# Two blocks in f32: the last expert's rows added by TensorE, scores between query tiles, and the residual's last addition moved ahead

## The chip, the cores and the metric

One core of one Trainium2 chip runs the kernel. The metric is the device time of one execution in microseconds, lower is better. The kernel before took 2692.67 us (median of 3 runs, 2691.4 to 2695.11).

## The reference, cut to what matters

Everything is f32, 256 tokens of 1024 features. Two layers of a hybrid mixer, a cross-attention to a memory of 256 rows and a feed-forward part (dense in layer 0, eight experts with the best two per token in layer 1); then a second block (mLSTM, linear recurrence, and a retrieval of 16 x 8 single-neuron experts per token).

```python
def memory_cross_attention(xn, memn, w_xq, w_xkv, w_xo):     # 4 heads of 256
    q = (xn @ w_xq).reshape(bsz, s, X_HEADS, X_HEAD_DIM)
    k, v = jnp.split(memn @ w_xkv, 2, axis=-1)
    ...
    scores = jnp.einsum("bshd,bmhd->bhsm", q, k).astype(jnp.float32) * (X_HEAD_DIM ** -0.5)
    p = jax.nn.softmax(scores, axis=-1).astype(v.dtype)
    o = jnp.einsum("bhsm,bmhd->bshd", p, v).reshape(bsz, s, D_MODEL)
    return o @ w_xo

def moe_swiglu(xn, w_router, w_gate, w_up, w_down):
    ...
    for e in range(N_EXPERTS):
        y = y + combine[:, e:e + 1] * swiglu(xt, w_gate[e], w_up[e], w_down[e])

h = h + memory_cross_attention(rmsnorm(h, norm_x_g[layer]), ...)
h = h + (swiglu(...) if layer % 2 == 0 else moe_swiglu(...))      # then rmsnorm, second block
```

## The kernel before, in words

The residual `hF` lies transposed in SBUF: features on partitions, 8 tiles (`KT`) of 128 features by 256 tokens. Every engine has its own program, written out by hand, and they meet in semaphores. TensorE's program (`pe`) is the first to be written; the class `Groups` numbers its accumulation groups, hands out the eight PSUM banks in two rings of four ("v" banks emptied by VectorE, "a" banks by ScalarE), and remembers for each group the count at which it is done (`G.after`), the count at which it is taken (`G.took`), and which weight tile had been used by then (`G.tiles_at`). `G.begin` makes TensorE wait until the group four back in the same ring was taken.

Weights come in tiles of 1 MB, in a ring of seven, by SP's queue in the order in which they are used; a tile's load waits for the use of the tile seven before it. For most matrices a product is made of three: ScalarE rounds the tile to its high part (`round_ahead`, line 1489), VectorE subtracts to get the low part (`low_ahead`, line 1986), and TensorE multiplies high by high, low by high and high by low (`split_group`, lines 644, 645, 648; 48 matmul records for a group of 256 outputs). `round_ahead(key)` and `low_ahead(key)` first do every such tile up to `AHEAD` = 2 tiles behind the group `key`; they stand in front of the wait for that group, so the engine does tiles while TensorE works on it. An f32 matmul that is not split shows as two records.

**Attention** (`attention(l)` in each engine's program, both layers). TensorE: sums of squares, the last key-value tile, four query groups, then the four heads' scores (line 782), four groups of transposes of the probabilities, four output groups (line 794), then the output matrix `xo`. ScalarE copies the query groups to `qF` (line 1628), then for each head waits for the maximum and writes the exponentials with their sums (line 1641). VectorE takes the four maxima (lines 2174, 2175), then normalises head by head (2179, 2181), then copies the transposed probabilities (2187). Before the maxima it does `low_ahead((("q", l), 3))`.

**Residual.** `add_to_residual(key, follow)` on VectorE: per group g the low parts ahead, `follow(g - 1)`, then the addition of the group (line 2003). For `xo` the function to follow is `gained_low_parts` in layer 0 (low parts of the normalised input of the feed-forward, line 2025) and `gained_tokens` in layer 1 (line 2017). On ScalarE, `norm` squares each pair of tiles as it is added (line 1520), in layer 0 with the high parts of the scaled input (1523), and first does `round_ahead((h_key, g))`. TensorE sums the squares (line 554).

**Experts.** The tokens of an expert are listed by a matmul (buffer `lists`: tokens, shares and destination rows), POOL gathers their rows from `x_tokens` in DRAM, and TensorE transposes them; all this for the next expert while the current one runs. Behind the down projection ScalarE writes `ye` (tokens of this expert by 1024 features, scaled by their shares, line 1733), and POOL adds it to `y_tokens` in DRAM by an indirect DMA with an add (line 1449, signal `y_done`). `pick` is the one-hot matrix of tokens and places of the next expert; `weighted_now` is a copy of it made for the current one. After the last expert SP waits for `y_done` of all eight, reads 256 rows back (line 1370, `y_loaded`), TensorE transposes them in four groups, and VectorE adds them to the residual (line 2419). Then every engine skips the body of `If(overflow > 0)`, a second pass over all experts for lists longer than 128, and the second block starts: ScalarE's squares (1761), TensorE's sums (554), VectorE's `gain_sq` (2438), TensorE's sums with it (1009), VectorE's reciprocals (2445, 2450), rows of the next input (2453) and the first matrix (622). SP's next seven loads stand behind the read-back on its queue.

In the second block a padding transpose `pad_v` (VectorE's copy of it at 2636) is put in where the number of "v" groups so far is odd. The last stage is a run of 256 indirect gathers of rows by POOL, with row numbers in the buffer `work`.

## Time and profile before

| | us |
|---|---|
| median of 3 runs | 2692.67 |
| lowest, highest | 2691.4, 2695.11 |
| the profiled execution | 2696.5 |
| its span, to which all times of the trace refer | 2694.4 |
| busy in it: TensorE, VectorE, ScalarE, POOL | 2529.3, 2008.3, 1237.7, 286.4 |
| mean granted clock of TensorE | 0.975 |

A time in the trace counts from the span's start. The chain that ended last is followed back from the last instruction, at each step to what released it. "Issue" in it is time in which the engine waited for nothing that the profile shows. Matmuls overlap, so a record's length is more than the step from one to the next. The granted clock (PEclk) is 1.00 at 2.4 GHz and 0.50 at 1.2 GHz. In brackets stands how long the engine was idle before a row, and what released it.

### The profile page before, as it was taken

The page shows a single profiled execution, that of the slowest core. Times are in us where ns is not written, and L with a number is a line of the kernel's source. Part 1 is how long each engine was busy: PE and PEld are TensorE (multiplying, and loading weights), DVE is VectorE, ACT ScalarE, POOL GpSimd, SP SyncE. Part 2 cuts the span into 40 slices and gives each one's busy share as a digit, 9 for nine tenths or more (in the row PEclk, how much of TensorE's full clock was granted, in tenths as well). Part 3 has the DMA queues.
Part 4 walks back from the last instruction along what each step waited for, and adds up shares of the span by engine and source line. Part 5 has one row for each costly group of instructions (what it writes and reads, how often), then busy time and mean ns, then how long its engine had stood idle before and what let it go on. Part 6 is the DMA issues. An engine that isn't in the chain of part 4 may idle for free.

```text
span 2694.4 us, 33145 instructions
## 1 busy us (share of the span) xinstructions
PE 2529.3 (94%) x12345; PEld 1981.4 (74%) x12345; DVE 2008.3 (75%) x2983; ACT 1237.7 (46%) x1250; POOL 286.4 (11%) x303
## 2 busy tenths in 40 slices
PE   9999999999999999999999997999999987787787
PEld 7898999899788888888888886888896543333332
DVE  5765654864888898889889894537656878888875
ACT  1454331263778777777777783124532111021111
POOL 0000000000000000000000000000003443333331
PEclk9999999999999999999999998999999999888899
DMA  7553554551999999999999996432658999999997
GB/s 219 168 196 110 188 180 119 164 161 60 343 373 378 368 383 368 376 371 377 377 372 382 364 385 213 146 110 63 193 171 344 422 420 422 421 422 422 421 421 310
DMA packets 339200, 788.32 MB, mean 293 GB/s; under 512 B 22288, under 2 KB 154512, under 8 KB 306064
## 3 DMA queue, kind: packets, MB, share of 16 engines
q1 hardware_dynamic: 298352, 504.99, 53.4%
q0 software_dynamic: 39600, 278.41, 25.4%
q10 hardware_dynamic: 1136, 3.43, 0.3%
q8 instruction: 70, 1.15, 0.2%
q14 instruction: 42, 0.34, 0.0%
HBM read 778.92 MB, written 7.86 MB: 292 GB/s over the span
## 4 chain that ended last, share of the span: by engine, by line
PE 76%; DMA 14%; DVE 4%; issue 3%; ACT 3%; POOL 0%; DVEq 0%; SPq 0%; ACTq 0%; POOLq 0%
DMA dense_weights<-in_peer_rows,work 12%; PE banks L810 12%; PE banks L812 12%; PE banks L811 12%; PE banks L622 6%; PE banks L685 5%; PE banks L1228 5%; PE banks L644 4%; PE banks L648 4%; PE banks L645 4%; PE banks L1191 2%; PE banks L921 1%; PE banks L554 1%; DMA squares<-in_peer_rows,work 1%; ACT weight_tiles_high L1489 1%
## 5 line engine op out<-in xcount | busy, mean ns | idle before, releaser
L2319 DVE TENSOR_TENSOR weight_tiles_low<-weight_tiles,weight_tiles_high 128x2048 fp32r<-128x2048 f32 x335 | 763.1, 2288 | 99.1 <-ACT weight_tiles_high L1701 97.3
L1701 ACT ACTIVATE weight_tiles_high<-weight_tiles 128x2048 fp32r<-128x2048 f32 x332 | 636.2, 1918 | 193.4 <-DMA weight_tiles<-in_moe_w_down 73.1
L1228 PE MATMUL banks<-dense_weights,work 128*128 128x512 f32 x952 | 463.0, 640 | 107.5 <-DVE work L2721 107.5
L1228 PEld LDWEIGHTS banks<-dense_weights,work 128*128 128x128 f32 x952 | 188.9, 204 | 369.9 <-issue 214.9
L810 PE MATMUL banks<-weight_tiles_high,gathered_parts 128*128 128x512 f32 x896 | 352.7, 394 | 1.3 <-DVE gathered_parts L2330 1.3
L812 PE MATMUL banks<-weight_tiles_high,gathered_parts 128*128 128x512 f32 x896 | 349.3, 390 | 0.0
L811 PE MATMUL banks<-weight_tiles_low,gathered_parts 128*128 128x512 f32 x896 | 348.9, 389 | 0.0
L2711 DVE CUSTOM_DVE_ANT_0 dense_weights<-dense_weights,banks 128x1024 f32<-128x1024 f32 x238 | 285.4, 1217 | 70.5 <-DMA dense_weights<-in_peer_rows,work 69.2
L1468 POOL DMA_INDIRECT dense_weights<-in_peer_rows,work x238 | 223.7, 940 | 702.9 <-DVE work L2688 331.2
L1986 DVE TENSOR_TENSOR weight_tiles_low<-weight_tiles,weight_tiles_high 128x2048 fp32r<-128x2048 f32 x85 | 194.1, 2289 | 130.1 <-ACT weight_tiles_high L1489 129.9
L1907 ACT ACTIVATE work<-work,small 128x2 f32<-128x2 f32 x129 | 38.1, 295 | 538.3 <-DVE work L2711 529.1
L812 PEld LDWEIGHTS banks<-weight_tiles_high,gathered_parts 128*128 128x128 f32 x896 | 168.2, 188 | 35.6
L810 PEld LDWEIGHTS banks<-weight_tiles_high,gathered_parts 128*128 128x128 f32 x896 | 168.3, 188 | 35.3 <-issue 1.5
L811 PEld LDWEIGHTS banks<-weight_tiles_low,gathered_parts 128*128 128x128 f32 x896 | 168.4, 188 | 34.0
L1489 ACT ACTIVATE weight_tiles_high<-weight_tiles 128x2048 fp32r<-128x2048 f32 x85 | 161.9, 1906 | 59.0 <-PE banks L812 32.1
L810 PE MATMUL banks<-weight_tiles_high,work_parts 128*128 128x512 f32 x448 | 179.0, 400 | 0.0
L811 PE MATMUL banks<-weight_tiles_low,work_parts 128*128 128x512 f32 x448 | 176.9, 395 | 0.0
L812 PE MATMUL banks<-weight_tiles_high,work_parts 128*128 128x512 f32 x448 | 176.8, 395 | 0.0
L644 PE MATMUL banks<-weight_tiles_high 128*128 128x256 f32 x736 | 174.8, 281 | 0.0
L645 PE MATMUL banks<-weight_tiles_high,weight_tiles_low 128*128 128x256 f32 x736 | 174.1, 280 | 0.0
L622 PE MATMUL banks<-normed,weight_tiles 128*128 128x256 f32 x640 | 141.0, 380 | 1.5 <-DVE normed L2453 1.5
L644 PEld LDWEIGHTS banks<-weight_tiles_high 128*128 128x128 f32 x736 | 139.9, 190 | 0.2 <-issue 0.2
(445 smaller groups left out, 3833.0 us busy)
## 6 DMA issues: line engine op xcount, KB each, us to landing
weight_tiles<-in_moe_w_gate SPq DMA_DIRECT2D x112, 1024.0 KB, 7.0
weight_tiles<-in_moe_w_up SPq DMA_DIRECT2D x112, 1024.0 KB, 6.7
weight_tiles<-in_moe_w_down SPq DMA_DIRECT2D x112, 1024.0 KB, 6.0
weight_tiles<-in_w_in SPq DMA_DIRECT2D x38, 1024.0 KB, 5.8
weight_tiles<-in_w_xkv SPq DMA_DIRECT2D x16, 1024.0 KB, 5.6
weight_tiles<-in_ffn_w_gate SPq DMA_DIRECT2D x11, 1024.0 KB, 5.3
weight_tiles<-in_ffn_w_up SPq DMA_DIRECT2D x11, 1024.0 KB, 5.3
weight_tiles<-in_ffn_w_down SPq DMA_DIRECT2D x11, 1024.0 KB, 4.9
```

Of the source, the lines that this page charges most:

```text
L622: mm = pe.matmul(bank[:, i * SEQ:(i + 1) * SEQ], w[:, k, i * P:(i + 1) * P], x(k), start=(k == 0), stop=(k == KT - 1))
L644: pe.matmul(o, high[:, k, n_], high_x(k), start=(k == 0 and i == 0), stop=False)
L645: pe.matmul(o, low[:, k, n_], high_x(k), start=False, stop=False)
L810: pe.matmul(o, a_high, b_high, start=start, stop=False)
L811: pe.matmul(o, a_high, b_low, start=False, stop=False)
L812: return pe.matmul(o, a_low, b_high, start=False, stop=stop)
L1228: mm = pe.matmul(halves[half], diag[(first + j) % 8], pair_row(first + j)[:, 1, half * 512:(half + 1) * 512], start=False, stop=end and j ...
L1468: pool.indirect_dma_start(out=pair_row(c).rearrange("p t d -> p (t d)"), out_offset=None, in_=t["peer_rows"], in_offset=bass.IndirectOffse ...
L1701: act.activation(high_tile(j), raw_tile(j), ACT.Copy).then_inc(g.high, 1)
L1986: dve.tensor_tensor(low_tiles[:, n % RING, 0:size], raw_tiles[:, n % RING, 0:size], high_tiles[:, j % HIGH_RING, 0:size].bitcast(F32), ALU ...
L2319: dve.tensor_tensor(low_tile(j), raw_tile(j), high_tile(j).bitcast(F32), ALU.subtract).then_inc(g.split, 1)
L2711: ins = dve.tensor_tensor_reduce(u_row, u_row, tokens(b), 1.0, 0.0, ALU.mult, ALU.add, dots[:, c:c + 1])
```

## The change

1. The last expert's rows are no longer scattered by POOL. The read-back waits for seven scatters and for the last expert's token transposes. TensorE transposes `weighted_now` to `put`, VectorE copies it, TensorE transposes the rows read back, and multiplies `ye` by `put` in four groups, which VectorE adds to the residual.
2. In the attention of both layers the scores of head h are computed behind query group h + 1; ScalarE's copies and VectorE's maxima, normalisings and low parts are interleaved to match.
3. At `xo` the last group's addition no longer waits for the low part of a further tile and for `follow(2)`; ScalarE's last round ahead falls away there in layer 0.
4. The buffer `lists` is allocated last.

```diff
@@ -251,14 +251,14 @@
         rstd_row = sb("rstd", [P, SEQ])
         eps = sb("eps", [P, 1])
         router = sb("router", [P, KT, N_EXP])
-        lists = sb("lists", [P, 16])
-        x_tokens = nc.dram_tensor("x_tokens", [SEQ, D], F32).ap()
-        y_tokens = nc.dram_tensor("y_tokens", [CLEARS * P, D], F32).ap()
         small = sb("small", [P, 256])
         extra_flag = sb("extra_flag", [P, 1], I32)
         WORK = 13848
         work = sb_under("work", [P, WORK])
         work_parts = sb("work_parts", [P, WORK], F32R)
+        lists = sb("lists", [P, 16])
+        x_tokens = nc.dram_tensor("x_tokens", [SEQ, D], F32).ap()
+        y_tokens = nc.dram_tensor("y_tokens", [CLEARS * P, D], F32).ap()
         def view(off, *shape, extra=False):
@@ -651,11 +651,17 @@
    def split_linear(key, who, x, dmas=1):
+       for g in split_groups(key, who, x, dmas):
+           pass
+
+   def split_groups(key, who, x, dmas=1):
+
        for g in range(4):
            tile = split_tile(KT, 2 * P, dmas)
            bank = G.begin(who, (key, g))
            G.end(split_group(bank, tile, (P, P), *x))
            G.free()
+           yield g
    pe.wait_ge(ones_ready, 1)
    bank = G.begin("a", "warm")
@@ -773,15 +779,19 @@
        norm_sums(("x_ms", l))
        key_value(l, 7)
        seen.next("x")
-       split_linear(("q", l), "a", normed_split())
-       pe.wait_ge(act_took, G.took[("q", l), 3])
-       for h in range(HEADS):
+       def scores(h):
+           pe.wait_ge(act_took, G.took[("q", l), h])
            bank = G.begin("a", ("scores", l, h))
            for b in range(TB):
                for j in range(2):
                    mm = pe.matmul(bank[:, b * SEQ:(b + 1) * SEQ], qF[:, 2 * h + j, b * P:(b + 1) * P],
                                   kF[:, 2 * h + j, :], start=(j == 0), stop=(j == 1))
            G.end(mm)
+
+       for g in split_groups(("q", l), "a", normed_split()):
+           if g > 0:
+               scores(g - 1)
+       scores(HEADS - 1)
        for h in range(HEADS):
            pe.wait_ge(probs_ready, HEADS * l + h + 1)
            transposes("v", ("probsT", l, h), [(m * SEQ + b * P, probs[:, h, b, m * P:(m + 1) * P])
@@ -990,9 +1000,18 @@
    overflow = pe.value_load(extra_flag[0:1, 0:1], min_val=0, max_val=1)
    experts(0)
    G.experts_done = G.total
+   transposes("v", "put", [(b * P, weighted_now[:, b, :]) for b in range(TB)])
    pe.wait_ge(y_loaded, 16)
    for i in range(KT // 2):
        transposes("v", ("y", i), [(j * SEQ + b * P, y_rows[:, b, (2 * i + j) * P:(2 * i + j + 1) * P]) for j in range(2) for b in range(TB)])
+   pe.wait_ge(dve_took, G.took["put"])
+   for i in range(KT // 2):
+       if i % 2 == 0:
+           pe.wait_ge(act_took, G.took["down", i // 2] + (N_EXP - 1) * G.takes["a"])
+       bank = G.begin("v", ("scatter_last", i))
+       for j in range(2):
+           mm = pe.matmul(bank[:, j * SEQ:(j + 1) * SEQ], ye[:, (2 * i + j) * P:(2 * i + j + 1) * P], put, start=True, stop=True)
+       G.end(mm)
    G.given_moe = G.given["v"]
    with pe.If(overflow > 0):
        for who in "va":
@@ -1366,7 +1385,8 @@
    resume = n
    sp.wait_ge(*G.before_experts)
    experts(G)
-   sp.wait_ge(y_done, 16 * (CLEARS + N_EXP))
+   sp.wait_ge(y_done, 16 * (CLEARS + N_EXP - 1))
+   sp.wait_ge(group_done, G.after["gather", KT // 2 - 1] + (N_EXP - 1) * G.in_turn)
    sp.dma_start(y_rows, y_tokens[0:SEQ, :].rearrange("(b p) d -> p b d", p=P)).then_inc(y_loaded, 16)
    more = passes[1]
    with sp.If(overflow > 0):
@@ -1445,6 +1465,8 @@
        pool.wait_ge(g.took_sems["v"], g.took["lists"] + e * g.takes["v"])
        pool.indirect_dma_start(out=x_rows, out_offset=None, in_=x_tokens,
                                in_offset=bass.IndirectOffsetOnAxis(ap=token_at, axis=0)).then_inc(rows_gathered, 16)
+       if e == N_EXP - 1:
+           break
        pool.wait_ge(g.took_sems["a"], g.took["down", 1] + e * g.takes["a"])
        pool.indirect_dma_start(out=y_tokens, out_offset=bass.IndirectOffsetOnAxis(ap=put_at, axis=0), in_=ye, in_offset=None,
                                compute_op=ALU.add).then_inc(y_done, 16)
@@ -1515,7 +1537,8 @@
        for g, (dst, src) in enumerate(square_parts()):
-           round_ahead((h_key, g))
+           if gain is None or g < 3:
+               round_ahead((h_key, g))
            act.wait_ge(dve_took, G.took[h_key, g])
            act.activation(dst, src, ACT.Square).then_inc(sq_ready, 1)
            if gain is not None:
@@ -1632,8 +1655,14 @@
        round_x()
        ready(("kv", l, 7))
        take(act.activation(vM[:, :, 3 * 256:D], pair(banks_of(("kv", l, 7))), ACT.Copy))
-       copies(("q", l), qF)
+       def query(h):
+           ready((("q", l), h))
+           take(act.activation(qF[:, 2 * h:2 * h + 2, :], pair(banks_of((("q", l), h))), ACT.Copy))
+
+       query(0)
        for h in range(HEADS):
+           if h + 1 < HEADS:
+               query(h + 1)
            act.wait_ge(max_ready, HEADS * l + h + 1)
            bank = banks_of(("scores", l, h))
            for b in range(TB):
@@ -1995,13 +2024,15 @@
    def add_to_residual(key, follow=None):
        for g in range(4):
-           low_ahead((key, g))
-           if follow is not None and g > 0:
+           if follow is None or g < 3:
+               low_ahead((key, g))
+           if follow is not None and 0 < g < 3:
                follow(g - 1)
            ready((key, g))
            s = hF[:, 2 * g:2 * g + 2, :]
            take(dve.tensor_tensor(s, pair(bank_of((key, g))), s, ALU.add))
        if follow is not None:
+           follow(2)
            follow(3)
    def gained_rows(g):
@@ -2166,14 +2197,7 @@
    def attention(l):
        norm(("x_ms", l), lambda k: c_vec(l, X_G, k))
        split_x()
-       low_ahead((("q", l), 3))
-       for h in range(HEADS):
-           ready(("scores", l, h))
-           bank = banks["a"][(G.took["scores", l, h] - 1) % 4]
-           s = small[:, h * TB:(h + 1) * TB]
-           step.now(dve.tensor_reduce(s, pair(bank), AX.X, ALU.max))
-           dve.tensor_scalar(s, s, -(HD ** -0.5), None, ALU.mult).then_inc(max_ready, 1)
-       for h in range(HEADS):
+       def normalise(h):
            dve.wait_ge(act_took, G.took["scores", l, h])
            r = small[:, 16 + h * TB:16 + (h + 1) * TB]
            step.now(dve.reciprocal(r, small[:, 8 + h * TB:8 + (h + 1) * TB]))
@@ -2182,6 +2206,17 @@
                if b < TB - 1:
                    step.then(ins)
            ins.then_inc(probs_ready, 1)
+
+       for h in range(HEADS):
+           low_ahead((("q", l), min(h + 1, 3)))
+           ready(("scores", l, h))
+           bank = banks["a"][(G.took["scores", l, h] - 1) % 4]
+           s = small[:, h * TB:(h + 1) * TB]
+           step.now(dve.tensor_reduce(s, pair(bank), AX.X, ALU.max))
+           dve.tensor_scalar(s, s, -(HD ** -0.5), None, ALU.mult).then_inc(max_ready, 1)
+           if h > 0:
+               normalise(h - 1)
+       normalise(HEADS - 1)
        for h in range(HEADS):
            ready(("probsT", l, h))
            take(dve.tensor_copy(probsT[:, h, :, :], pair(bank_of(("probsT", l, h)))))
@@ -2413,10 +2448,15 @@
    dve.wait_ge(routing_ready, 1)
    overflow = dve.value_load(extra_flag[0:1, 0:1], min_val=0, max_val=1)
    experts(0)
-   for i in range(KT // 2):
-       ready(("y", i))
-       s = hF[:, 2 * i:2 * i + 2, :]
-       take(dve.tensor_tensor(s, pair(bank_of(("y", i))), s, ALU.add))
+   ready("put")
+   take(dve.tensor_copy(put, bank_of("put")[:, 0:SEQ]))
+   for name in ("y", "scatter_last"):
+       for i in range(KT // 2):
+           ready((name, i))
+           if name == "scatter_last":
+               dve.wait_ge(dve_took, G.took["y", i])
+           s = hF[:, 2 * i:2 * i + 2, :]
+           take(dve.tensor_tensor(s, pair(bank_of((name, i))), s, ALU.add))
    with dve.If(overflow > 0):
        experts(1)
```

## Rows read from the trace of the kernel before

**Rows 1.** The page, part 4: chain that ended last, shares by engine.
```profile
PE 76%; DMA 14%; DVE 4%; issue 3%; ACT 3%; POOL 0%; DVEq 0%; SPq 0%; ACTq 0%; POOLq 0%
```

**Rows 2.** Chain that ended last, behind the experts: start us, length us, what.
```profile
1650.43 1.32 ACT work L1733 x2
...
1652.01 6.65 DMA y_tokens<-work,lists
...
1658.68 5.55 DMA work<-y_tokens
...
1664.27 3.69 PE banks L546 x16
...
1668.06 5.57 issue
1673.63 2.15 DVE work L2438 x8
...
1675.82 6.65 PE banks L1009 x16
```

**Rows 3.** Timeline there, by engine: start us, us, engine, line, operation [idle before <-releaser].
```profile
1593.29 38.51 SPq L1351 DMA_DIRECT2D weight_tiles<-in_moe_w_down  x14
...
1664.61 15.40 SPq L1300 DMA_DIRECT2D weight_tiles<-in_w_in  x7
...
1667.98 0.69 DVE L2419 TENSOR_TENSOR residual<-banks,residual 128x512 f32<-128x512 f32 x1 [0.16 <-PE banks L546]
...
1668.40 3.69 PE L554 MATMUL banks<-squares,ones 128*128 128x256 f32 x16 [0.46 <-issue]
```

**Rows 4.** Timeline of the attention, layer 0, by engine.
```profile
197.58 7.17 PE L782 MATMUL banks<-dense_weights,work 128*128 128x256 f32 x32 [0.69 <-ACT work L1628]
206.46 3.54 PE L546 MATMUL banks<-ident,work 128*128 128x128 f32 x16 [1.71 <-DVE work L2181]
...
209.79 7.48 PE L794 MATMUL banks<-squares,dense_weights 128*128 128x256 f32 x32
...
204.79 0.69 DVE L2174 TENSOR_REDUCE small<-banks 128x2 f32<-128x512 f32 x1 [0.83 <-PE banks L782]
...
205.78 0.62 DVE L2181 TENSOR_SCALAR work<-work,small 128x256 f32<-128x256 f32 x2
...
205.72 0.47 ACT L1641 ACTIVATE work<-banks,small 128x256 f32<-128x256 f32 x1 [0.71 <-DVE small L2175]
```

**Rows 5.** Timeline of TensorE, attention, layer 1.
```profile
629.71 2.69 PE L546 MATMUL banks<-ident,work 128*128 128x128 f32 x12 [1.70 <-DVE work L2181]
```

**Rows 6.** Timeline of the feed-forward's entry, layer 0, by engine.
```profile
240.14 2.75 PE L554 MATMUL banks<-squares,ones 128*128 128x256 f32 x12
245.42 1.13 PE L554 MATMUL banks<-squares,ones 128*128 128x256 f32 x4 [2.52 <-ACT squares L1520]
...
241.02 2.29 DVE L1986 TENSOR_TENSOR weight_tiles_low<-weight_tiles,weight_tiles_high 128x2048 fp32r<-128x2048 f32 x1 [3.30 <-ACT weight_tiles_high L1489]
```

**Rows 7.** Chain that ended last, feed-forward's entry, layer 0.
```profile
244.10 0.61 DVE residual L2003
244.74 0.64 ACT squares L1520
...
247.02 0.12 PE banks L644
```

**Rows 8.** Windows of 1 us: busy of PE, PEld, DVE, ACT, POOL, then PEclk, DMA, GB/s.
```profile
208.00:209.00 1.00, 1.00 (x7) 1.00 (x6) 1.00 (x3) 0.00 (x0) 0.00 (x0) 0.50 0.00 0
...
1675.00:1676.00 1.00, 0.18 (x1) 0.18 (x2) 1.00 (x6) 0.00 (x0) 0.00 (x0) 0.50 1.11 351
```

**Rows 9.** Timeline of TensorE before the output matrix of the second block.
```profile
1980.68 1.04 PE L546 MATMUL banks<-ident,weight_tiles 128*128 128x128 f32 x8
...
1985.18 0.81 PE L546 MATMUL banks<-ident,weight_tiles 128*128 128x128 f32 x4 [2.55 <-DVE small L2636]
```

**Rows 10.** Timeline of TensorE, router logits.
```profile
663.40 3.63 PE L847 MATMUL banks<-router,normed 128*128 128x8 f32 x32
```

## The prediction

> **What bounds the kernel now.** I read the chain that ended last first: three quarters of the span is TensorE [rows 1], so what can be won before the last stage is the time in which TensorE stands still, and work taken off it. The last stage (row gathers) waits for transfers and comes after all four edits, so a microsecond won earlier is a microsecond of the end, as long as a gather keeps its price. I then read the chain and the timeline of the places that the diff touches.
>
> Seam behind the experts: the last two activations that write `ye` end at 1651.75, the scatter by indirect DMA takes 6.65 us, the read-back 5.55, the transposes 3.69, then come 5.57 us of "issue" before VectorE's next instruction, its 2.15 us of `gain_sq`, and the sums of line 1009 [rows 2]. "Issue" there is VectorE: its last residual addition (0.69) starts at 1667.98, behind it stands the skipped overflow branch, and line 2438 starts at 1673.63 [rows 2, 3].
>
> Attention, layer 0: TensorE waits 0.69 us for the last query copy, runs all scores in 7.17, waits 1.71 for the softmax of head 0, transposes in 3.54 and forms the outputs in 7.48, to 217.27 [rows 4]. Layer 1 repeats it (1.70 us) [rows 5]. Feed-forward entry: the first 12 matmul records of the norm's sums end at 242.89, and TensorE waits 2.52 us for the last squares, because the last addition ends at 244.7 only, behind a tile's low part that VectorE starts at 241.02 and two gained rows [rows 6, 7].
>
> **Part 1, the last scatter on TensorE.** Removed from the path: scatter 6.65 and read-back 5.55. The read-back moves into the last expert: it now waits for seven scatters and that expert's token transposes, both early in or before its down projection, and stands on SP's queue behind the last expert tile, issued at 1631.8 [rows 3]; TensorE works on to 1651, so 5.55 us lie under it. What stood behind the read-back on SP's queue, the next stage's seven loads (issued at 1664.61 [rows 3]), now starts when the experts end; they are first used after the norm, so this is cover, not gain.
>
> Added on TensorE behind the last down matmul, which ends about 1651.1 (the second of two activations of 0.66 us starts there [rows 2]): 2 + 16 transposes. At the full clock 8 took 1.04 us [rows 9], so 18 take 2.3: to 1653.4. VectorE copies `put` (half as wide as an addition of 0.69 [rows 3], so at most that) and makes four such additions, to about 1654.8, just ahead of the banks' next users. Then 8 matmuls of 128x128x256 in f32, each two records; 32 records took 7.17 [rows 4], so 16 take 3.6: the last group ends at 1657.0, where the last y group ended at 1667.96 (1664.27 + 3.69 [rows 2]). The four new additions follow their groups as the old ones did. VectorE's branch, `gain_sq` and all behind move with that group: **gain 11.0 us.**
>
> What could be late next is ScalarE: it too skips the branch, and before it did so under 14 us of waiting. I price its skip by VectorE's 5.57: free at 1657.3, four squares of about 0.64 [rows 7] to 1659.9, the last sums 0.9 us later, table load and square root under 2 more: about 1662.6, while `gain_sq` ends only at 1657.0 + 5.65 + 2.15 = 1664.8. Hidden by 2 us. TensorE's own sums ran 0.5 us behind the transposes with squares already there [rows 3]: its skip, begun at 1664.3 at the earliest, was over by 1668.40, so at most 4.1 us; the same after 1654.8 ends at 1658.9, plus 3.69 is 1662.6, also hidden.
>
> Bounds: with the granted clock at 0.50 the same kind of work took 6.65 for 16 records [rows 2] and 3.69 for 16 transposes, and both parts at that level give only 6.5 us. Above: line 1009 itself ran at 0.50 after TensorE's wait [rows 8]; if the shorter wait left it at full clock it would take 3.69 instead of 6.65, 14 us in all. I take 11.0: before the 0.50 stretches the engine had stood still for 1.7 us or more [rows 4, 8], and in the new seam it does not.
>
> The Trainium skill, page "Runtime: NRT & Kernel Launch", section "Instruction fetch mechanics", says that a taken branch whose target is outside the fetched window forces a fetch before execution goes on. By that every engine pays at the skip, ScalarE and TensorE too, and with all three fetches now falling in a few microseconds beside the weight loads it speaks against this part; the trace agrees for VectorE (5.57), and the rival below takes it up.
>
> **Part 2, scores between query tiles** (both layers). The 7.17 us of scores stay; two heads' worth (3.6) moves ahead of the last two query tiles. With the end of the last query tile as zero (196.9 = 197.58 - 0.69), before: outputs done at 20.4. After: scores 2 and 3 to 3.6 (the last query copy, 0.6, lies under scores 2, so the wait of 0.69 is gone); maximum 0.9 with its scaling, two exponentials 1.0, normalising 0.8 with its reciprocal [rows 4] to about 6.4; last transposes 0.55 to 7.0; outputs at full clock 7.17 to 14.2. With the moved 3.6 that is 17.8, so 2.6 a layer. On ScalarE, rounding of the output matrix's tiles is now queued behind the exponentials of heads 0 and 1, and on VectorE their low parts behind the maxima of heads 0 and 1; each head takes 1 to 2 us of either engine, a tile 2.3 [rows 6], and a query group on TensorE (48 records, one every 0.12 us [rows 7]) more than 5, so the tiles come in time. The exponential's table load now falls in a query tile. Bounds: TensorE still waits in two pieces of about 0.6 us for heads 2 and 3; if that draws the 0.50 clock for as long as before (about 3 us; its level stands in [rows 8]), 1.5 us are lost and 1.0 is left; nothing if VectorE's queue turns out late. Near the upper end, since 1.7 us in one piece become two short ones: 2.2 each, **4.4 us.**
>
> **Part 3, the last addition first** (layer 0). VectorE no longer does a tile's low part (2.29 [rows 6]) and two gained rows before the last addition. The output group ends at about 240.3 (its sums' records start there [rows 6]); addition 0.69 and square 0.64 end at 241.7, before TensorE has done the 12 records at 242.89. So the whole wait goes, no more: **2.5 us.** The low part comes afterwards: ScalarE rounds that tile before its square root (about 244.4), VectorE subtracts to 246.7, and TensorE needs it one group (5.7 us) after 243.9. The reciprocal follows it and is done a little before the first group ends at 249.6. Lower bound 1.5, were it late. In layer 1 only the gained rows change places: the rows of tiles 4 and 5 come 0.6 us later than possible, under logits that take 3.63 us in order of tiles [rows 10]. Zero.
>
> **Part 4, what rides along.** The list buffer moves behind `work_parts`: all behind it shift by 64 bytes, no instruction changes: zero. Five more VectorE groups turn the count's parity, so the padding transpose before the keys falls away; TensorE waited 2.55 us for its copy [rows 9], but the next group's bank comes free only one key copy later, so I take **0.3**.
>
> Sum: 11.0 + 4.4 + 2.5 + 0.3 = 18.2 us. The profiled execution took 2696.5 (span 2694.4), 3.8 above the median; I take the gain from the median: 2692.7 - 18.2 = 2674.5.
>
> **Rivals.**
> A, the clock falls (0.13): transposes and small waits hold TensorE at 0.50 through both seams. Part 1 gives 6.5, part 2 2.0, parts 3 and 4 2.8: 11.3 us, 2681.4. For it: the stretches at 0.50 in just such places [rows 8]. Against: a long wait stood before each.
> B, the skip is bared (0.12): three fetches beside 1 MB loads. If each took 10 us, VectorE would lose 4.4, part 1 would be 6.6 and the sum 13.8: 2678.9. For it: VectorE's 5.57. Against: its fetch was already beside the loads, issued 3.4 us before it, and the weights' phase to it hardly changes.
> C, slower (0.03): the shift of `work`, which holds the gathers' row numbers, makes a gather dearer. The last stage issues 256 gathers one after the other, and the chain runs through them [rows 1]. At 18.2 / 256 = 0.07 us more for each the whole gain is gone; at 0.1 us each the stage is 25.6 us longer and the end 7.4 us later than before: 2700.1. For it: only that the stage's length hangs on many small transfers. Against: nothing in an instruction changes but a base address.
> D, an edit does nothing (0.04), for instance the softmax order stalls a query tile on VectorE's queue and part 1 is partly hidden: under 5 us, 2689.
>
> Forecast 0.68. Its own range comes from part 1 at 9 to 14, part 2 at 2 to 5.2, part 3 at 1.5 to 2.5: 2671 to 2680; with A and B, and two microseconds of scatter between runs, 2669 to 2683. No measurement of this kernel can tell 0.2% (5.4 us) from no change; faster by more takes in the forecast, A and B.
>
> **What would show it.** Right: no indirect write behind the last expert and the read-back inside it; a first `gain_sq` about 5.6 us after the last scatter group and 11 us nearer to `ye`; waits of 0.69 and 1.71 gone in both layers; line 554 without its 2.52. Wrong: TensorE waiting for `ye`, for `put` or for the read-back; squares starting later than their additions by microseconds and `gain_sq` no longer last; granted clock 0.50 in the scatter; a query tile waiting for VectorE; a gather stage longer than before.

## The result and the profile after

| | before | after |
|---|---|---|
| median of 4 runs, us | 2692.28 | 2660.32 |
| lowest, highest | 2691.4, 2695.11 | 2659.57, 2661.13 |
| span of the profiled execution | 2694.4 | 2658.4 |
| its mean granted clock | 0.975 | 0.981 |

The ratio is 0.988, its 95% interval 0.9862 to 0.9897. The change takes 32.0 us off; I had forecast 18.2, and the time lies 8.7 us under the range's lower end. The three mechanisms of the forecast are in the trace, and together worth 19.5 us there for the 17.9 forecast. Most of the rest came from the edit that I had priced at zero. The two profiled spans differ by more, 36.0 us: the profiled execution of before took 2696.5 us and lies 4.2 over its median, that of the kernel after lies at its median.

The page's part 4 of the kernel after, the shares of the chain by engine, against [rows 1]: still TensorE.

```profile
PE 77%; DMA 14%; DVE 4%; issue 2%; ACT 2%; POOL 0%; ACTq 0%; DVEq 0%
```

The seam behind the experts, timeline of the kernel after, by engine (start us, length us, engine, line, operation, [idle before <-releaser]), against [rows 2, 3]:

```profile
1627.01 0.38 PE L546 MATMUL banks<-ident,squares 128*128 128x128 f32 x2
1627.22 1.91 PE L546 MATMUL banks<-ident,work 128*128 128x128 f32 x16
1628.97 3.62 PE L1013 MATMUL banks<-squares,work 128*128 128x256 f32 x16
1637.07 6.43 PE L554 MATMUL banks<-squares,ones 128*128 128x256 f32 x16 [4.48 <-issue]
1643.34 3.62 PE L1028 MATMUL banks<-squares,work 128*128 128x256 f32 x16
...
1651.41 1.97 PE L622 MATMUL banks<-normed,weight_tiles 128*128 128x256 f32 x8 [1.55 <-DVE normed L2493]
...
1627.43 0.42 DVE L2452 COPY squares<-banks 128x256 f32<-128x256 f32 x1 [9.74 <-PE banks L546]
1627.86 3.73 DVE L2459 TENSOR_TENSOR residual<-banks,residual 128x512 f32<-128x512 f32 x6
...
1632.63 0.69 DVE L2459 TENSOR_TENSOR residual<-banks,residual 128x512 f32<-128x512 f32 x1 [0.17 <-PE banks L1013]
1639.16 2.14 DVE L2478 TENSOR_SCALAR work<-ones,cols 128x128 f32<-128x128 f32 x8 [5.84 <-issue]
...
1633.35 0.63 ACT L1790 ACTIVATE squares<-residual 128x512 f32<-128x512 f32 x1 [0.23 <-DVE residual L2459]
...
1643.54 0.47 ACT L1528 ACTIVATE std<-banks,eps 128x256 f32<-128x256 f32 x1 [8.26 <-PE banks L554]
...
1608.63 0.40 SPq L1390 DMA_DIRECT2D work<-y_tokens  x1
1627.20 31.75 SPq L1319 DMA_DIRECT2D weight_tiles<-in_w_in  x8
```

To be seen: the read-back is issued at 1608.63, inside the last expert. The four scatter groups (L1013) begin behind the transposes without a wait and end at 1632.59. TensorE then stands 4.48 us with nothing to wait for, which is its skipped overflow branch, and the norm's 16 records take 6.43. The square root starts when they end (1643.54); the `gain_sq` products of VectorE had been ready at 1641.3 (1639.16 + 2.14). From the last down matmul's end to the next stage's first matmul it was 35.9 us (1651.0 to 1686.9) and is 24.2 (1627.2 to 1651.41): 11.7 less. This stretch, called the seam below, varies between executions: in the eleven traces of this case with the old order it took 33.0 to 35.9 us (mean 35.0), in the five with the new order and nothing added 23.0 to 24.2 (mean 23.6).

Windows of 1 us there, columns as in [rows 8]: half the clock behind the 4.48 us, the full clock from 1643 on.

```profile
1640.00:1641.00 1.00, 1.00 (x3) 0.78 (x3) 1.00 (x6) 0.00 (x0) 0.00 (x0) 0.50 1.28 283
...
1645.00:1646.00 1.00, 1.00 (x7) 0.87 (x6) 0.80 (x1) 0.00 (x0) 0.00 (x0) 1.00 1.10 357
```

Attention and feed-forward entry, layer 0, TensorE, against [rows 4, 6]:

```profile
199.77 3.61 PE L787 MATMUL banks<-dense_weights,work 128*128 128x256 f32 x16
203.22 1.04 PE L546 MATMUL banks<-ident,work 128*128 128x128 f32 x8
205.08 0.66 PE L546 MATMUL banks<-ident,work 128*128 128x128 f32 x4 [0.83 <-DVE work L2205]
206.27 0.66 PE L546 MATMUL banks<-ident,work 128*128 128x128 f32 x4 [0.53 <-DVE work L2205]
206.96 7.15 PE L804 MATMUL banks<-squares,dense_weights 128*128 128x256 f32 x32
...
236.56 3.62 PE L554 MATMUL banks<-squares,ones 128*128 128x256 f32 x16
```

The waits of 0.69 and 1.71 have become 0.83 and 0.53 for heads 2 and 3, and the outputs run at full clock (7.15 for 7.48). From the start of the query tiles to the first matmul of the output projection it was 41.97 us in either layer, and is 39.45 (174.30 to 213.75) and 39.46: 2.5 less each. The norm's sums at the entry run through in 3.62, and the stretch from their start to the first gate record is 3.26 us (236.56 to 239.82) for 6.06: 2.8 less. In the eleven traces without the third edit this stretch took 6.1 to 7.4 us, in the six with it 3.3 each time.

That makes 11.7 + 5.0 + 2.8 = 19.5 of the 36.0 us between the two spans. The rest is in no wait at all. In long stretches without a gap TensorE starts its matmuls closer together. Two rows of each kernel show it; the records between them (three before, four after) are left out. Timeline of TensorE in the down projection of an expert, kernel before:

```profile
790.29 0.40 PE L810 MATMUL banks<-weight_tiles_high,work_parts 128*128 128x512 f32 x1
...
791.22 0.40 PE L811 MATMUL banks<-weight_tiles_low,work_parts 128*128 128x512 f32 x1
```

and after:

```profile
784.99 0.39 PE L820 MATMUL banks<-weight_tiles_high,work_parts 128*128 128x512 f32 x1
...
786.12 0.39 PE L822 MATMUL banks<-weight_tiles_high,work_parts 128*128 128x512 f32 x1
```

Before, four steps in 0.93 us, 233 ns each; after, five in 1.13, 226 ns each. The records' own lengths (0.40 and 0.39) hardly tell: matmuls overlap, so the step from start to start is what counts. By whole stretches (first to last start, divided by the steps; the experts' rows hold the step of about 0.32 us behind each group of transposes, without which they are 227.3 and 227.1 for gate and up, 233.3 and 227.3 for down):

```
stage (steps)                       before            after
expert, gate and up (2640)          228.6 ns          228.5 ns     longer pauses left out
expert, down (1320)                 234.8             228.9        longer pauses left out
feed-forward gate and up (1055)     118.0             113.5
feed-forward down (527)             120.1             117.9
output projection, layers 0 and 1   120.9, 120.9      118.8, 114.4
```

The experts take 963.8 us before (687.24 to 1651.01) and 955.7 after: 8.1. The feed-forward's gate and up give 4.7, its down projection 1.2, the two output projections 1.7, the mixers and keys 1.6, the second block 0.5; the routing of layer 1 costs 1.1 more. 19.5 + 8.1 + 4.7 + 1.2 + 1.7 + 1.6 + 0.5 - 1.1 = 36.2, the 36.0 within the rounding of its terms.

The routing is longer through the clock. The router's logits took 3.63 us before and take 4.27, the norm's sums behind them 5.39 and 6.41: the granted clock is 0.68 in the window from 649 to 650 us and 0.50 from there to 656, though TensorE had run up to it without a gap, since 646.55 with the 8-column matmuls of the logits. Three of the four traces of programs with all four edits show it (logits 4.27 to 4.60), the fourth doesn't (3.64), nor do those with some of the edits.

### The profile page after: what moved, and what is told of

Read it like the earlier page. It is cut to its first block, busy times and chain, and to the rows that moved or that the text cites. A ratio compares the mean times of both kernels' runs of the same rounds, so it can differ in the third digit from the quotient of the medians.

```text
span 2658.4 us, 33195 instructions
## 1 busy us (share of the span) xinstructions
PE 2504.0 (94%) x12362; PEld 1967.7 (74%) x12362; DVE 2010.2 (76%) x2987; ACT 1237.4 (47%) x1250; POOL 286.5 (11%) x302
## 4 chain that ended last, share of the span: by engine, by line
PE 77%; DMA 14%; DVE 4%; issue 2%; ACT 2%; POOL 0%; ACTq 0%; DVEq 0%
DMA dense_weights<-in_peer_rows,work 12%; PE banks L820 12%; PE banks L822 12%; PE banks L821 12%; PE banks L622 6%; PE banks L691 6%; PE banks L1247 5%; PE banks L644 4%; PE banks L648 4%; PE banks L645 4%; PE banks L1210 2%; PE banks L554 1%; PE banks L931 1%; DMA squares<-in_peer_rows,work 1%; DVE work L2761 1%
```

## The experiments

Theory after the result: the list buffer's move shifts `small`, the flag and the work region by 64 bytes, and TensorE's pace depends on where its operands begin. Rivals: the new order of instructions sets the pace; or the pace differs from one execution to the next, and the result is a lucky draw.

**Parts one by one.** First the list buffer alone:

```diff
-        lists = sb("lists", [P, 16])
         small = sb("small", [P, 256])
 ...
         work_parts = sb("work_parts", [P, WORK], F32R)
+        lists = sb("lists", [P, 16])
```

> The kernel before with the list buffer allocated last and nothing else; work and work_parts move down by 64 bytes. Theory A (an operand's address sets TensorE's pace, and a stretch's pace is handed on to the next): all the pace gain is here, about 16 us: expert matmuls with work_parts at 227 ns instead of 233 (8 us in the experts), xo 118 or less, feed-forward gate and up at 113 instead of 118 (4.8 us); median about 2676. Theory B (the address acts only where an operand lies in work_parts; the rest comes from when a stretch starts, which the other edits moved): experts 8 us, feed-forward down 1.2, gate and up unchanged at 118; median about 2682. Theory C (my prediction: nothing): 2692.

Then everything but that (the changed kernel with the hunk above taken back):

> The changed kernel with the list buffer where it was before; the three edits of the program stay. Theory A: the mechanical gains alone, about 18 to 19 us, experts again 964 us, feed-forward gate and up again 118 ns; median about 2674 to 2676. Theory B: experts 964 us but gate and up at 113 ns, median about 2669. Prediction: 2674.5.

Hunks of the last expert alone, then of the scores alone, then of the last addition alone:

> The kernel before with only the last expert's scatter on TensorE. Time from the last down matmul to the first matrix of the second block 24.2 us instead of 35.9, so 11.7 less; the padding transpose gone too (0.3). Paces as before everywhere up to the seam under either theory. Median about 2680. If the seam's gain needs the other edits: less than 10.

> The kernel before with only the scores between query tiles. Both theories: 2.5 us less in each attention between the start of query group 0 and the end of the outputs, 5 in all. Theory B (start moments set the pace): query group 2 at 118 as in the changed kernel, and a changed pace in xo or in the feed-forward (113 instead of 118, 4.8 us more gained) is possible; theory A: xo 120, feed-forward 118 as before. Median 2687 by A, 2682 by B.

> The kernel before with the third edit alone: in the feed-forward's entry the residual's last addition comes ahead of the others, and its skip matches. By the prediction's sum (2.5) and by the stretch from the last output to the first gate matmul in the two traces (6.06 us before, 3.26 after) this is worth 2.8 us: 2689.5. The experts keep 963.8 us, since no buffer moves. If the layer-0 gate and up matmuls' pace (118 ns before, 113 ns with either of the two other edits alone and with both) follows the code or the moment of entry, it may change here too and take 4.8 us more off; if it varies from one execution to the next, this run says little and the repeat of the kernel before says more.

```
                     median us   less than before   ratio, 95%          experts us  gate/up ns  down ns
lists alone          2682.05     10.2               0.9953 to 0.9978    955.6       118         113
all but the lists    2673.8      18.5               0.9922 to 0.9955    963.8       113         120
last expert alone    2683.1       9.2               0.995  to 0.9978    963.8       113         120
scores alone         2687.67      4.6               0.9976 to 0.9995    963.8       113         120
addition alone       2688.27      5.5               0.9965 to 0.9984    963.8       113         120
```

(2692.27 before for the first four, 2693.72 for the last.) The move of the buffer alone gives 10.2 us, though no instruction changes; all but the move gives 18.5, and stands at 2673.8 where the forecast said 2674.5. The experts' stage is 955.6 or 963.8 in these five, according to the list buffer and to nothing else. Gate and up are another thing: 113 ns in all four without the move and 118 with it alone, so the move, if anything, does not speed them up.

The seam without the move, timeline of TensorE in the kernel with all but the lists:

```profile
1640.32 3.62 PE L1013 MATMUL banks<-squares,work 128*128 128x256 f32 x16
1648.42 5.16 PE L554 MATMUL banks<-squares,ones 128*128 128x256 f32 x16 [4.48 <-issue]
...
1661.48 2.83 PE L622 MATMUL banks<-normed,weight_tiles 128*128 128x256 f32 x12 [1.55 <-DVE normed L2493]
```

The same 4.48 us of issue, 5.16 for the sums: 23.0 us from 1638.5 to 1661.48. With the last expert's edit alone it is 23.0 too, where I had expected 24.2. The seam's gain doesn't hang on the addresses.

**The same program again.** The kernel before, unchanged:

> The kernel before, unchanged, with a profile of its own. If the pace of the layer-0 gate and up matmuls (118 ns in the first profile) is a matter of each execution, it can come out at 113 ns here, and the span with it 4.8 us shorter; if it is fixed by the code, it is 118 ns again. The experts must be 963.8 us and the down projection 120 ns again.

Gate and up, TensorE's timeline of the first profile of before, eight records apart:

```profile
299.86 0.28 PE L644 MATMUL banks<-weight_tiles_high 128*128 128x256 f32 x1
...
300.80 0.28 PE L644 MATMUL banks<-weight_tiles_high 128*128 128x256 f32 x1
```

and of the second, six apart:

```profile
300.24 0.28 PE L644 MATMUL banks<-weight_tiles_high 128*128 128x256 f32 x1
...
300.92 0.28 PE L644 MATMUL banks<-weight_tiles_high 128*128 128x256 f32 x1
```

0.94 / 8 is 118 ns, 0.68 / 6 is 113 ns: one program, two paces, held from the second of 22 tiles to the last (124.7 and 120.0 us for the stage). The experts (963.8) and the down projection (120 ns) were alike in both. Expected either way, and it settles that one program draws either pace, so the 4.7 us of gate and up between the two spans need no effect of the change. In the 17 traces of this case the stage ran at 118 ns seven times and at 113 ten times. These draws and those of the seam can account for a good part of before's 8 us of scatter.

**Which operand.** The first suspicion was the high half of the expert's hidden tile, the stationary operand of the down projection: with the buffers laid out in order of their allocation it begins at byte 195776 of a partition before and at 195712 after. It can be moved by one constant, while all buffers stay. The same constant places what lies behind it in the region: the low half (14336 bytes on, so with the same remainder by 256), the unrounded tile and `ye`.

```diff
-HE_AT, Y_AT, HID_AT, O_HIGH_AT = 5456, 7680, 0, 4096
+HE_AT, Y_AT, HID_AT, O_HIGH_AT = 5472, 7680, 0, 4096
```

> The kernel before with nothing changed but where inside the work region the high half of the expert's hidden tile begins: 64 bytes later (5456 to 5472 elements). All the buffers stay where they were. Theory (the 128-byte alignment of that tile, which is the stationary operand of the down projection, sets 234 or 227 ns per 512-column matmul): the experts' stage falls from 963.8 to 955.6 us, the time by 8.2 to about 2684, and the feed-forward's down projection and the output projections keep their 120 ns, as their operands haven't moved. Rival (the place of another buffer that moved with the lists, such as the lists themselves or the small tiles, sets it): the experts stay at 963.8 us and the time at 2692.

A miss: 962.8 us of experts, 233.1 ns in the long stretches, 2694.11 us (ratio 0.9992 to 1.0011). A line of 128 bytes is not the rule. But the pace moved by 1 ns, so I tried the other direction in the kernel before (`HE_AT` 5440) and the old address in the changed kernel (5472):

> The kernel before with the expert's hidden tile 64 bytes earlier inside the work region (5456 to 5440 elements). Its high half then begins at the very address (byte 195712 of a partition) that it has in the changed kernel; nothing else has moved. If the address of that stationary operand sets the pace of the down projection, the experts fall from 963.8 to 955.6 us. If they stay at 963.8, it isn't that operand's address, and the lists, the small tiles or the base of the work region are left.

> The changed kernel with the expert's hidden tile 64 bytes later inside the work region (5456 to 5472 elements), so that its high half begins at the address (byte 195776) that it has in the kernel before. If that address sets the pace, the experts rise from 955.7 to 963.8 us and the time from 2660.3 to about 2668.5; if something else that moved with the lists sets it, they stay at 955.7.

Kernel before with the tile at 195712, five steps:

```profile
785.05 0.39 PE L810 MATMUL banks<-weight_tiles_high,work_parts 128*128 128x512 f32 x1
...
786.18 0.39 PE L812 MATMUL banks<-weight_tiles_high,work_parts 128*128 128x512 f32 x1
```

Changed kernel with the tile at 195776, five steps:

```profile
779.77 0.40 PE L820 MATMUL banks<-weight_tiles_high,work_parts 128*128 128x512 f32 x1
...
780.94 0.39 PE L822 MATMUL banks<-weight_tiles_high,work_parts 128*128 128x512 f32 x1
```

1.13 against 1.17 us: 955.6 us of experts in the first, 963.7 in the second. The place of this tile, high and low half together, carries the whole difference of the experts' stage, in both kernels and both ways. No other buffer that moved with the lists is needed. Which of the two halves counts was not tried. For the period of the rule, `HE_AT` 5504 (byte 195968):

> The kernel before with the expert's hidden tile at 5504 instead of 5456 elements: its high half begins at byte 195968, 256 bytes behind 195712, where the pace was 227.9 ns. If the rule repeats every 256 bytes the experts come out at 955.6 us; if it repeats every 512 (the other operand that ran at 227.0 ns, the gathered tokens at 139904, has the same residue of 512 as 195712, and so have the weights) they stay at about 963.8.

955.5 us, 227.6 ns: 256 bytes on the fast pace is back, so the period is 256 bytes in this pair of places. Two more, which move the work region's base by 32 and 96 bytes (flag last; lists and flag last):

> The kernel before with only the one-word flag buffer behind the work region, which thus begins 32 bytes earlier (residue 96 of 128); the lists and the small tiles keep their places. If the work region's base is what counts, and any place off a 128-byte line will do, the output projections of layer 0 and the feed-forward's down projection leave 120 ns for 118 or 113, and the experts fall below 963.8 us. If the lists' place counts, nothing changes: 120 ns, 963.8 us.

> The kernel before with the lists and the flag behind the work region, which begins 96 bytes earlier (residue 32 of 128); the small tiles 64 bytes earlier. If every place off a 128-byte line will do, it goes like the lists alone (experts 955.6, down projection 113 or 118 ns, about 2682 us); if residue 64 is needed, the experts come out between 955.6 and 963.8 or above, and the 120 ns stay.

Both keep 963 us of experts (1644.10 - 681.09, 1647.45 - 684.59); the output projections and the feed-forward's down projection come to 117 to 119 ns, neither 120 nor 113. All places together, with the mean of the 107 steps behind each expert's last transposes (the first of them is 0.32 us long and adds 0.8 ns):

```
stationary operand, 512 moving columns      remainder of 256     long stretches
gathered tokens, every kernel   139904      128                  227.1 to 227.3 ns, single steps
lists alone, after              195712      128                  227.6 ns
before with HE_AT 5440          195712      128                  227.9
before with HE_AT 5504          195968      128                  227.6
lists and flag last             195680       96                  234.0
flag last                       195744      160                  234.0
before; after with HE_AT 5472   195776      192                  234.1
before with HE_AT 5472          195840        0                  233.1
```

These variants ran once each, so their times, against 2691.21 and 2692.52 us of before measured beside them, say little: `HE_AT` 5440 took 2689.19 us, 5504 took 2686.45, flag last 2689.1, lists and flag last 2694.89. The changed kernel with 5472 took 2674.37, 6 us more than I had expected; its experts' stage cost the 8.0 us expected, and gate and up (4.7) had drawn the slow pace. The argument goes by the stages in the traces.

**The moving operand.** The 120 ns of the output projection, with only the rounded attention output moved (`O_HIGH_AT` 4080 for 4096, byte 190272 for 190336, remainder 64 for 128):

> The kernel before with the rounded attention output 64 bytes earlier inside the work region (4096 to 4080 elements); everything else stays. It is the moving operand of two of three matmuls of the output projection. If the place of the moving operand (residue 64 rather than 0 of 128) is what freed the output and down projections from 120 ns, those two of three leave 120 for 113 or 118 ns, and each output projection takes 0.3 to 0.9 us less than its 23.4; the third, whose operand has not moved, keeps its pace or is drawn along. If not, all stay at 120 ns and 23.4 us. The experts stay at 963.8.

Output projection, layer 0, kernel before, eight steps:

```profile
225.02 0.28 PE L644 MATMUL banks<-work_parts,weight_tiles_high 128*128 128x256 f32 x1
...
225.98 0.28 PE L644 MATMUL banks<-work_parts,weight_tiles_high 128*128 128x256 f32 x1
```

and with the operand moved, eight steps:

```profile
225.02 0.28 PE L644 MATMUL banks<-work_parts,weight_tiles_high 128*128 128x256 f32 x1
...
225.93 0.28 PE L644 MATMUL banks<-work_parts,weight_tiles_high 128*128 128x256 f32 x1
```

0.96 against 0.91 us: 120 and 113 ns. The third matmul of each set (L648), whose operand had not moved, came to 118.7 ns on average for 120.0, and the projection took 22.5 us for 23.4 (22.7 in layer 1). The run took 2694.51 us, a single one. So the place of the moving operand sets the pace of the output projection's matmuls, and this is what the list buffer did to it. For the feed-forward's down projection, whose moving operands went from remainder 128 to 64 with the whole region, the same is argued, not shown alone.

**The half clock in the seam.** Fourteen matmuls into a bank nobody reads, ahead of TensorE's branch:

```diff
+            warm_bank = banks["a"][G.given["a"] % 4]
+            for _ in range(14):
+                pe.matmul(warm_bank[:, 0:P], ones[:, :], ones[:, :], start=True, stop=True)
             with pe.If(overflow > 0):
```

> The changed kernel with fourteen matmuls of ones by ones into a bank that nobody reads, put right ahead of TensorE's branch over the overflow part. Theory (the clock fell because TensorE stood idle between the scatter's end and the norm's sums): the sums of the final norm take about 3.7 us rather than 6.43, the seam between the experts and the second block shrinks by about 2 us, and the time is about 2658.3. Rival (the idle time that lets the clock fall is that of the branch itself, 4.5 us long, and the matmuls ahead of it only fill time that nobody waits for): the sums take 6.4 us again and the time is 2660.3 or up to 0.5 more.

```profile
1630.11 3.62 PE L1013 MATMUL banks<-squares,work 128*128 128x256 f32 x16
1633.56 3.29 PE L1018 MATMUL banks<-ones 128*128 128x128 f32 x28
1641.49 6.20 PE L554 MATMUL banks<-squares,ones 128*128 128x256 f32 x16 [4.64 <-issue]
...
1655.59 0.67 PE L622 MATMUL banks<-normed,weight_tiles 128*128 128x256 f32 x2 [1.54 <-DVE normed L2496]
```

The rival holds, and more. The 28 records take 3.3 us, the issue time behind them is still 4.64, the sums still 6.20, and the seam is 27.3 us (1628.3 to 1655.59) instead of 24.2: here work put ahead of the branch is paid in full. 2665.22 us (ratio to before 0.9872 to 0.9905), slower than the changed kernel. It shows that the pause at TensorE's skip is on the path now. (The medians differ by 4.9, the seams by 3.1; the rest is within what the two-level stages do, and gate and up ran at 118 ns here.)

The pause is not simply the price of the branch. In the six traces with the new order TensorE stands 4.26 to 4.64 us behind its last matmul; in the eleven with the old order, behind 16 transposes and ahead of the same branch, it stood 0.6 us or less, and the sums started 3.6 to 4.3 us behind the start of those transposes. So the skip ran under the transposes there, and here it doesn't run under the scatter nor under the filling matmuls. What makes the difference no run shows.

**Does the result hold?** The changed kernel once more:

> The changed kernel once more, unchanged, timed on this chip. The experts must be 955.7 us again and the seam behind them 24.2. The stages with two levels may come out at either: gate and up 120.0 or 124.7 us, down 60.1 or 62.4, output projections 22.1 or 23.0. The median should be 2660.3, up to 2665 where the slower levels come more often, as the first four runs were few.

2660.24 us, 2658.05 to 2662.19, ratio 0.9857 to 0.989. Experts 955.7, gate and up 120.0, down 62.4, output projections 23.0 and 23.0, where the first profile had 22.1 in layer 1. The 32 us stand.

## Why the prediction was wrong

**The step that failed** is the zero of "Part 4": "all behind it shift by 64 bytes, no instruction changes: zero". It is worth 10.2 us alone (0.9953 to 0.9978), 8.2 of it in the experts. I took it for granted that a matmul's price doesn't depend on its operands' addresses, and even had the edit's address shift in hand as rival C, but asked only what it does to the gathers, and only as a loss. It did no harm there: the first gather starts 35.8 us earlier (2024.88, 1989.06) and the end comes 36.0 earlier. The rows could have warned me. The timeline of before has two kinds of expert matmuls with equal shapes and engines, at 227 and at 233 ns, and query and output projections at 113 and at 120. An edit that moves buffers has its bound in that spread: 1344 steps of about 6.5 ns are 8.7 us.

**Part 1, forecast 11.0, measured 11.7.** The read-back is hidden, nobody waits for `put` or the transposes, the scatter runs at full clock, and its last group ends 5.4 us behind the last down matmul, against 5.9 forecast. What I had wrong is what comes last. I wrote that TensorE's skip would take "at most 4.1 us" and its sums 3.69, "also hidden". It takes 4.48 behind the scatter's end, not behind 1654.8 in the old times: the scatter's matmuls stand ahead of the branch in TensorE's order, and I started the skip at the transposes. My "at most 4.1" was read from a place where the skip ran beside the transposes. Then the sums run at half the clock, and end 10.9 us behind the scatter (1632.59 to 1643.51), while `gain_sq` is done 8.7 behind it. What paid that back is the next group of sums, which took 6.65 us at half the clock before (line 1009 [rows 2]) and now, behind sums without a pause, 3.62 (L1028). From the end of the last group to the first matrix it was 18.96 us and is 18.82: the bared skip and the slow sums cost 3.1, the full clock returned 3.0. That 11.7 lies so near 11.0 is thus luck in part, two errors that cancel. Rival B, the bared skip, is thus true for TensorE and untrue in its price: VectorE's took 5.84 for 4.95 before (the 5.57 of the forecast counts from inside its last addition), and ScalarE's, which I had priced at 5.57, fits under the 3.08 us between `ye` and the first square. The Trainium skill, page "Runtime: NRT & Kernel Launch", section "Instruction fetch mechanics", says that a taken branch whose target lies outside the fetched window forces a fetch before execution goes on. The 4.26 to 4.64 us of TensorE in the new order agree with it; the 0.6 us or less in the old order don't show it, for there the skip was hidden.

**Part 2, forecast 4.4, measured 5.0.** The two short waits are there (0.83 and 0.53, I had two of 0.6) and did not draw the half clock, so my upper end of 2.6 a layer was the better value. Alone it gave 4.6 us, 0.9976 to 0.9995.

**Part 3, forecast 2.5, measured 2.8** in this pair of traces, and 2.8 to 4.2 against the other traces without it; alone 5.5, 0.9965 to 0.9984, an interval of 4.3 to 9.4 us that has the draws of the two-level stages in it. For layer 1 I had forecast zero; alone it was zero (logits 3.63 us), with all four edits the routing cost 1.1 in the pair. Rival A is out as I put it: the clock was full in the scatter, in the attention's end and at the entry. But it fell in the norm's sums behind the scatter and in the routing, there with no pause ahead of it, so my argument that a standstill of 1.7 us or more must come first does not hold. D is out: each of the three edits of the program gave something. **The padding transpose, forecast 0.3, measured nothing**: its wait of 2.55 us is gone, but TensorE now waits 3.12 ahead of the matrix instead, and from the first transpose with a tile to the matrix it is 5.4 us for 5.1.

**The sum** of the mechanical parts was right within 1.3 us: 18.2 forecast, 18.5 by the medians without the list move, 19.5 by the stretches. The range failed since none of my cases let a bare address matter on the good side. What stays open: 10.2 + 18.5 leave 3.3 of 32.0 us, inside the intervals of the two; why a stage without address or order changed holds 113 in one execution and 118 in the next; why TensorE's skip hid under the old transposes and not under the new scatter; and whether the output and down projections can be made to take 113 each time. No version here beats the changed kernel.

## What to carry to other kernels

When an edit adds, removes or reorders a buffer, list which matmul operands behind it change place, and compare the steps from start to start of matmuls of equal shape before you price it at zero: here 3% of a step hung on it, 8 us of the kernel, and one constant sets it. A record's length doesn't show it; the step between starts does. And look at what stands directly ahead of a skipped branch in an engine's own order: a skip that hides in the old order (0.46 us of pause) can show in the new one (4.48), and here filling work put ahead of it was paid in full.

## What the runs showed that I had not expected

- With a stationary operand that begins 128 bytes past a multiple of 256, matmuls of 512 columns ran at 227 to 228 ns a step; at remainders 0, 96, 160 and 192 they took 233 to 234. Remainders 32 and 64 weren't tried. All moving tiles began at remainder 128 too, so whether it is the stationary operand's own place or its place against the moving one's stays open. 512 columns were the only width tried.
- Matmuls of 256 columns with weights as stationary operand took 120 ns a step with the moving operand at remainder 128, 113 or 118 at 64, and 117 to 119 at 32 and 96. By moving the operand alone this was shown for remainders 128 and 64 only.
- Stages at remainder 64 have two levels, 113 and 118 ns, and the gate and up projections kept one from their second tile to their end; the same program drew either for the gate and up projections, a difference of 4.7 us. The stages at 120 ns (output and down projections, remainder 128) drew no other level in any trace.
- At the branch that it skips TensorE paused 4.26 to 4.64 us in the six traces of the new order, and the 16 records behind took 5.2 to 6.4 us for 3.6 at full clock; in the eleven of the old order it paused 0.6 us or less.
- The granted clock fell to half inside the router's logits though TensorE had run without a gap ahead of them, in three of four traces of the changed program.
